# A fused decoder layer on one core: head weights scaled one step sooner, values copied by bank, one instruction less in the last root

## What is computed

```python
return gb[..., 0:1] * o_c + gb[..., 1:2] * o_s + gb[..., 2:3] * o_w
```

```python
h = h + y @ w_o[l]
n = rmsnorm(h, mlp_norm_w[l])
h = h + jnp.square(jax.nn.relu(n @ w_up[l])) @ w_down[l]
return rmsnorm(h, final_norm_w)
```

## Time and profile before

| | us |
|---|---|
| runs of the kernel before | 1051.05, 1051.85, 1051.92 (median 1051.85) |
| the profiled execution, its own time | 1051.07 |
| its span, first to last instruction | 1049.3 |
| granted TensorE clock, mean | 0.997 of full speed |
| PE busy | 1036.7 |
| PEld (weight loads, beside PE) busy | 896.3 |
| DVE busy | 637.0 |
| ACT busy | 503.4 |
| POOL busy | 92.5 |

### The profile page before, as it was taken

One profiled execution on the slowest core, in us unless ns is written; L12 is line 12 of the kernel. 1 busy time (PEld: TensorE's weight loads), 2 busy tenths in 40 slices (PEclk: granted clock), 3 DMA queues, 4 the chain that ended last, 5 costly groups with the idle time before them and its releaser, 6 DMA issues.

```text
span 1049.3 us, 14380 instructions
## 1 busy us (share of the span) xinstructions
PE 1036.7 (99%) x5631; PEld 896.3 (85%) x5631; DVE 637.0 (61%) x761; ACT 503.4 (48%) x630; POOL 92.5 (9%) x152
## 2 busy tenths in 40 slices
PE   8999999999999999999999999999999999999996
PEld 7889999888888888888888888888888888888885
DVE  4655976988856564565456556545554555655666
ACT  5645855977754543344334443334434433433434
POOL 2135100633200100000000000000000000000002
PEclk9999999999999999999999999999999999999998
DMA  9576672343346566566556655665566565656662
GB/s 330 181 209 199 210 242 81 142 141 97 105 130 192 162 196 188 182 195 199 185 180 195 198 180 187 195 198 183 181 197 196 182 185 196 196 177 189 198 201 80
DMA packets 89137, 190.42 MB, mean 181 GB/s; under 512 B 8758, under 2 KB 29964, under 8 KB 88716
## 3 DMA queue, kind: packets, MB, share of 16 engines
q1 hardware_dynamic: 88668, 189.41, 57.3%
q10 hardware_dynamic: 432, 0.52, 0.2%
HBM read 187.82 MB, written 2.10 MB: 181 GB/s over the span
## 4 chain that ended last, share of the span: by engine, by line
PE 95%; DVE 2%; ACT 1%; issue 0%; DMA 0%; DVEq 0%; ACTq 0%
PE ps L1805 23%; PE ps L1387 15%; PE ps L1388 15%; PE ps L1391 15%; PE ps L1808 12%; PE ps L1678 1%; PE ps L1679 1%; PE ps L1682 1%; PE ps L1662 1%; PE ps L1635 1%; PE ps L1460 1%; PE ps L1663 1%; PE ps L1513 1%; PE ps L1512 1%; PE ps L1511 1%
## 5 line engine op out<-in xcount | busy, mean ns | idle before, releaser
L885 DVE TENSOR_TENSOR w_lo<-raw,w_hi 128x2048 fp32r<-128x2048 f32 (+4 forms) x198 | 402.4, 2034 | 355.3 <-ACT w_hi L594 289.3
L594 ACT ACTIVATE w_hi<-raw 128x2048 fp32r<-128x2048 f32 x119 | 228.1, 1917 | 399.3 <-PE ps L1391 200.7
L1805 PE MATMUL ps<-xT,w_hi 128*128 128x512 f32 x1024 | 279.4, 394 | 0.0
L1805 PEld LDWEIGHTS ps<-xT,w_hi 128*128 128x128 f32 x1024 | 176.1, 189 | 24.2
L1808 PEld LDWEIGHTS ps<-xT,w_lo 128*128 128x128 f32 x1024 | 157.2, 189 | 21.7
L1388 PE MATMUL ps<-w_lo,hidT 128*128 128x512 f32 x448 | 174.6, 390 | 0.0
L1387 PE MATMUL ps<-w_hi,hidT 128*128 128x512 f32 x448 | 174.6, 390 | 0.0
L1808 PE MATMUL ps<-xT,w_lo 128*128 128x256 f32 x1024 | 162.9, 281 | 0.0
L1391 PE MATMUL ps<-w_hi,hidT 128*128 128x512 f32 x448 | 138.2, 390 | 0.0
L587 ACT ACTIVATE w_hi<-raw 128x1024 fp32r<-128x1024 f32 (+3 forms) x75 | 104.2, 1392 | 67.9 <-PE ps L1391 40.9
L1391 PEld LDWEIGHTS ps<-w_hi,hidT 128*128 128x128 f32 x448 | 84.1, 188 | 17.6
(11 more groups left out here) (339 smaller groups left out, 1267.5 us busy)
## 6 DMA issues: line engine op xcount, KB each, us to landing
raw<-in_w_up SPq DMA_DIRECT2D x64, 1024.0 KB, 5.3
raw<-in_w_down SPq DMA_DIRECT2D x64, 1024.0 KB, 5.5
raw<-in_w_o SPq DMA_DIRECT2D x16, 1024.0 KB, 5.5
raw<-in_w_in SPq DMA_DIRECT2D x8, 1024.0 KB, 5.3
raw<-in_w_in SPq DMA_DIRECT2D x8, 816.0 KB, 4.5
raw<-in_w_in SPq DMA_DIRECT2D x6, 832.0 KB, 9.0
raw<-in_mla_w_uq SPq DMA_DIRECT2D x12, 256.0 KB, 4.6
raw<-in_mla_w_ukv SPq DMA_DIRECT2D x4, 512.0 KB, 4.9
```

The source lines that it names most:

```text
L594: act.activation(w_hi[:, j % SPLIT, :], raw[:, j % RAW, :], ACT.Copy).then_inc(hi_done, 1)
L885: return dve.tensor_tensor(dst, src, high.bitcast(F32), ALU.subtract)
L1805: pe.matmul(both, w_hi[:, slot, 512 * b + P * f:512 * b + P * f + P], xT[:, :, k0 + b, :], start=start and b == 0, stop=False)
```

## The change

Three edits.

1. The copy of the MLA values becomes two copies, bank 4 and then bank 5, each with its own signal. PE waits for the first before the products in bank 4 and for the second before those in bank 5.
2. `weights` of an NSA head is called at the end of DVE's "win" step (step i of the head's own two) instead of in the middle of the step after it. The MLA heads keep their place.
3. `root` gets half the rest ready before it waits for the last partial sum, and then makes `minus` in one instruction. The wait for `fsq` moves into `root`.

```diff
             dve.wait_ge(w_used, UKV_V + 1)
-            dve.tensor_copy(v_sb[:, 0, :], flat[:, 2048:3072]).then_inc(v_out, 1)
+            for n in range(2):
+                dve.tensor_copy(v_sb[:, 0, 512 * n:512 * n + 512], bank(4 + n)).then_inc(v_out, 1)
...
-                if 0 <= i - 2 < len(STEPS):
-                    weights(STEPS[i - 2][0], STEPS[i - 2][2], SOFT.get(i - 2))
+                if 0 <= i - 2 < NMLA:
+                    weights("mla", STEPS[i - 2][2], SOFT[i - 2])
                 if i - 2 in PIECES:
                     piece_weights(PIECES[i - 2])
...
                     low(yT[:, u, 1, :], ysb[:, u % 2, :], yT[:, u, 0, :], wcols[:, PRM["y"] + u:PRM["y"] + u + 1]).then_inc(y_lo, 1)
+                if kind == "win":
+                    weights("slc", h, SOFT[i - 1])
...
-            def root(t, part, rest, done):
+            def root(t, part, rest, before, done):
...
-                y, w, minus, mean = rc[:, t:t + 1], rc[:, 2 + t:3 + t], root_w[:, t:t + 1], root_w[:, 2 + t:3 + t]
-                link(dve.scalar_tensor_tensor(out=mean, in0=part, scalar=1.0 / D, in1=rest, op0=ALU.mult, op1=ALU.add))
-                link(dve.tensor_scalar(minus, mean, -0.5, None, ALU.mult))
+                y, w, minus, half = rc[:, t:t + 1], rc[:, 2 + t:3 + t], root_w[:, t:t + 1], root_w[:, 2 + t:3 + t]
+                link(dve.tensor_scalar(half, rest, -0.5, None, ALU.mult))
+                dve.wait_ge(fsq, before)
+                link(dve.scalar_tensor_tensor(out=minus, in0=part, scalar=-0.5 / D, in1=half, op0=ALU.mult, op1=ALU.add))
...
-            dve.wait_ge(fsq, 6)
-            root(1, ssq[:, 11:12], ssq[:, 14:15], root1)
+            root(1, ssq[:, 11:12], ssq[:, 14:15], 6, root1)
...
                 elif kind == "w":
                     if i == CMP[0]:
                         pe.wait_ge(blk_ok, 1)
-                        pe.wait_ge(v_out, 1)
                     y, half, s = CMP.index(i) // 2, CMP.index(i) % 2, split_slot(i)
+                    pe.wait_ge(v_out, y + 1)
```

More of the change, by code:

```diff
@@ L1337, in _ @@
             dve.wait_ge(rest_ok, 1)
-            dve.wait_ge(fsq, 3)
-            root(0, ssq[:, 13:14], ssq[:, 12:13], root0)
+            root(0, ssq[:, 13:14], ssq[:, 12:13], 3, root0)
             dve.wait_ge(last_t, 1)
```

## The result

| | before | after |
|---|---|---|
| median, us | 1051.85 (5 runs, 1051.05 to 1052.34) | 1056.02 (5 runs, 1055.74 to 1057.86) |
| the profiled execution, own time | 1051.07 | 1056.02 |
| its span | 1049.3 | 1054.2 |
| granted TensorE clock, mean | 0.997 | 0.998 |

What follows compares the result with a forecast made beforehand. PE, busy 99% of the span, bounds the kernel. Edit 1 -0.3, edit 3 -0.05 and edit 2 +1.95 sum to +1.6 us; against the median of 1051.85 the forecast was 1053.4 us, range 1051.2 to 1055.4.

Steps and rivals of the forecast that it cites:

- so the 0.3 us stay: After L1708: PE has no wait until the attention steps, so the split copy's gain of 0.3 us lasts.
- (a): Head 0: VectorE idles 1.5 us for exponentials, weights take 1.36, and the w_lo half behind delays PE by 0.1 us.
- The rival on GpSimd: Moved weights at heads 0 and 5 are slowed beside GpSimd's work: edit 2 costs 3.35, kernel 1054.85 us; chance 0.30.
- (b): Step 12: head 1's weights now precede `piece_in` on VectorE, so PE waits 0.6 us for the bank.
- (c): Step 17: head 3's weights, waiting for exponentials, precede the sum L1099, so PE waits 1.3 us.
- (d): Step 22: head 5's weights and an addition to h_sb precede `piece_in`, so PE waits 0.7 us.
- (e): Head 6: its weights are ready before PE asks, so PE's wait for them goes, -0.75 us.
- (f): From step 27 on: VectorE has idle room for the moved weights, so no cost.
- the waits at steps 13, 18 and 23: Sign of being right: PE idles 0.3 to 1.4 us before L1617 there, released by L1025 and L1099.
- w_lo as the main releaser: Sign of being wrong: PE's waits are mainly released by w_lo halves; no size given.
- The rival in which idling starves PE of w_lo: VectorE's idling delays w_lo halves at each of the first four heads: edit 2 costs 4 to 5, 1056 us; chance 0.05.
- The 0.05 for "faster": Whole kernel: chance 0.05 of being faster by over 0.2%, which would need 2.1 us.

## Why the prediction was wrong

I forecast +1.6 us on the median, within 0.2% of no change; it is +4.2, slower. The two profiled executions are 4.9 us apart, but 0.9 of that is the start phase (below), so trace and medians agree on about 4. The terms:

- **Edit 1**, -0.3 forecast, about 0 measured. The step "so the 0.3 us stay" failed: it read from the list that PE has no wait after L1708, but that list shows waits, not how nearly one was missed. `k2l` ended 0.18 us before PE's next load, and the pair of copies ahead of it takes 0.06 us longer than the one (1.28 against 1.22), so a gain of 0.43 us could keep hardly any. A reading was off as well: PE needs bank 5 not "some 4 us later" but 16 (the first product for the values starts at 132.09), so the second copy could have stood further back in VectorE's queue at no cost.
- **Edit 3**, -0.05 forecast, -0.06 measured alone. Right: the root is late next. In the full change the pair is 0.40 us apart (1047.93, 1048.33), but VectorE idles 0.36 us just before it, as in every kernel with the split copy, so nothing is won there.
- **(a) Head 0**, +0.1 forecast, +1.70 measured. This is the step that failed, by the sentence "these weights took 1.95 us ... I take 1.36 at the new place". The row of the trace said what weights cost in that stretch; I took the undisturbed price from elsewhere, although the exponentials that I had counted hold the block in that same stretch. The rival on GpSimd had the mechanism, and the pair of runs with small GpSimd work shows it. It was too small as well at head 0: it stretched one instruction by 0.6 us, and three were stretched, by 0.5, 0.5 and 0.3. Its other place, 0.8 us at head 5, did not come: those weights took 0.43 and 0.68 us (229.83, 230.17).
- **(b) Step 12**, 0.6 forecast, 0.2 measured; 0.5 without head 0. Right in place and cause; with PE held up by (a), most of it is covered.
- **(c) Step 17**, 1.3 forecast, 1.5 measured, plus 0.15 to 0.3 that PE's sum itself waited for head 3's masks, which I had not counted. **(d) Step 22**, 0.7 and 1.0. Right in place and cause, each a little small.
- **(e) Head 6**, -0.75 and -0.80. Right.
- **(f) After step 27**, nothing forecast, +0.2 measured (PE behind an addition to `h_sb` near 272 to 281). VectorE idles long there, as I wrote, but not at each place.

By my own signs: the waits at steps 13, 18 and 23 with L1025 and L1099 as releasers came, "w_lo as the main releaser" came too, and that sign stood under "wrong". The rival in which idling starves PE of w_lo gave a cost of 4 to 5 us, and the size fits it. But it wanted a starved half at each of four heads; there is one, at head 0, and without GpSimd beside it that one costs 0.3 us. So the time was near that rival's and the cause was not it. The 0.05 for "faster" belonged to none of my cases.

The Trainium skill ("SBUF — State Buffer", "Who interferes with whom") says that a VectorE instruction with two SBUF inputs and a GpSimd instruction that reads SBUF exclude each other. The rival that it stood beside had 0.30. The runs agree on who meets whom: all three stretched instructions read two SBUF tiles, and all three return to their plain durations when GpSimd's work is small. The masks of 128x256 read one SBUF tile and PSUM; in the changed kernel the 8 that overlap GpSimd's sums or bias tiles take 0.42 us in the mean, as do the 22 that overlap nothing of GpSimd's. That the later one waits for the whole of the first does not fit everywhere: the w_lo half began at 196.54, beside a bias instruction that ran until 197.65, and lost only 0.30 us.

## What to carry to other kernels

Before moving a block on an in-order engine, write down three things for every place it lands: what it waits for there, what stands behind it in the queue and who wants that soonest (readers of a bank and low halves above all), and what the same instructions take in that very stretch beside the other engines. If one instance of sixteen is waited for, move that one: head 6 alone gave the whole gain. A split copy pays only if its second half leaves the queue place of the next result that is wanted.

## What the hardware showed that I had not expected

The first 12 us differ between executions by up to 1.4 us, for kernels whose first 100 us are the same. In the pair of before and after it is the spacing of the first weight matmuls, which is wide at first and changes to the narrow one sooner or later. Kernel before, then the changed one, PE's timeline (groups of matmuls):

```profile
10.32 0.92 PE L1460 MATMUL ps<-w_lo,xT 128*128 128x512 f32 x4
11.08 0.60 PE L1432 MATMUL ps<-ident,x_sb 128*128 128x128 f32 x4
```

```profile
10.73 1.42 PE L1462 MATMUL ps<-w_lo,xT 128*128 128x512 f32 x4
11.99 0.60 PE L1434 MATMUL ps<-ident,x_sb 128*128 128x128 f32 x4
```

The difference of 0.91 us then stays unchanged until the first edit. Over the ten experiments it lay between -0.3 and +1.05 us and went with no edit. The granted clock reads 1.00 in that stretch in both, so the rows don't tell the cause. It is as large as the spread between most runs here, and it is why sub-microsecond edits had to be read from the start of the same matmul and not from times.
